# Sharing the samples' input projection with the prompt's, moving each second expert choice into the next window, and spreading the samples' last dots

## The reference

```
c -> modulation (6*1024 columns per layer, for the prompt and each sample)
h = RMSNorm(x) * (1 + scale1) + shift1
p = h @ w_in                                  (1024 x 3592, split into the three mixers' inputs)
A: dilated window attention, 4 heads x 64     (samples: against a cache of 2048 rows)
B: gated delta rule, 4 heads x 128, causal conv of width 4 on q/k/v
C: stick-breaking attention, 4 heads x 64     (samples: 16 cache pages of 128 rows each)
x += gate1 * (concat(A, B, C) @ w_out)
h2 = RMSNorm(x) * (1 + scale2) + shift2
q = h2 @ wq;  8 heads, scores against 2 x 128 keys, top 16 of 128 twice, top 16 of 256
x += gate2 * sum over 128 picks of softmax * gelu(h2 . u[idx]) * v[idx]     (16384 experts)
```

## Time and profile before

| what | value |
|---|---|
| runs of the kernel before | 4712.13, 4719.75, 4724.38 us; median 4719.75 |
| profiled execution | 4694.12 us, span of its instructions 4692.3 us |
| busy shares over the span | PE 73%, DVE 61%, POOL 55%, ACT 19% |
| moved by DMA | 1401.7 MB, mean 299 GB/s; gathers and other indirect loads 1107.4 MB of it |
| mean granted PE clock | 0.843 of full speed |

### The profile page before, as it was taken

One profiled execution on the slowest core, in us unless ns is written; L12 is line 12 of the kernel. 1 busy time (PEld: TensorE's weight loads), 2 busy tenths in 40 slices (PEclk: granted clock), 3 DMA queues, 4 the chain that ended last, 5 costly groups with the idle time before them and its releaser, 6 DMA issues. The chain is left out here.

```text
span 4692.3 us, 42307 instructions
## 1 busy us (share of the span) xinstructions
PE 3425.7 (73%) x11982; PEld 1910.2 (41%) x11982; DVE 2843.8 (61%) x5777; ACT 877.2 (19%) x2045; POOL 2587.5 (55%) x2244
## 2 busy tenths in 40 slices
PE   5966768539298889575887967498898436748897
PEld 2624543126154554262455426255553113213351
DVE  1225552556866648787774688868649767584322
ACT  1113110011142112112321211242221011000120
POOL 0000362025767757687774667777656767665563
PEclk8986789759589999796998988799999767869896
DMA  6451375549989989899998889999988989999995
GB/s 229 139 180 56 101 227 177 187 104 320 354 318 345 385 308 339 331 399 342 366 376 320 306 334 395 353 346 361 367 306 308 378 303 348 362 382 377 336 330 154
DMA packets 586674, 1401.71 MB, mean 299 GB/s; under 512 B 67314, under 2 KB 287659, under 8 KB 585244
## 3 DMA queue, kind: packets, MB, share of 16 engines
q0 software_dynamic: 306176, 1107.44, 63.6%
q1 hardware_dynamic: 261836, 274.77, 17.7%
q10 hardware_dynamic: 18432, 16.79, 1.1%
HBM read 1387.11 MB, written 11.88 MB: 298 GB/s over the span
## 5 line engine op out<-in xcount | busy, mean ns | idle before, releaser
L2496 PE MATMUL bank<-arena 128*128 128x512 f32 (+1 forms) x3264 | 1589.6, 636 | 200.5 <-PEq L2493 117.9
L2392 POOL DMA_INDIRECT arena<-in_peer_u_dram,arena x1056 | 1279.6, 1212 | 693.2 <-issue 303.1
L2392 POOL DMA_INDIRECT arena<-in_peer_v_dram,arena x1056 | 1160.5, 1099 | 749.2 <-PE bank L2496 448.4
L2442 DVE CUSTOM_DVE_ANT_0 arena<-arena 128x1024 f32<-128x1024 f32 (+1 forms) x1056 | 1269.8, 1224 | 447.5 <-DMA arena<-in_peer_u_dram,arena 417.4
L2496 PEld LDWEIGHTS bank<-arena 128*128 128x128 f32 (+1 forms) x3264 | 614.8, 196 | 1013.6 <-issue 869.5
L2479 ACT ACTIVATE arena<-arena 128x128 f32<-128x128 f32 (+1 forms) x816 | 301.5, 394 | 1072.9 <-PE bank L2496 686.1
L2458 DVE SCALAR_TENSOR_TENSOR arena<-arena 128x1024 f32<-128x1024 f32 x232 | 297.6, 1283 | 243.6 <-DMA arena<-in_peer_v_dram,arena 223.3
L799 PE MATMUL bank<-arena 128*128 128x256 f32 (+3 forms) x1472 | 368.9, 414 | 101.0 <-PEq L792 95.9
L2138 POOL DMA_INDIRECT arena<-in_cache_sb_k_dram,arena x64 | 84.0, 1312 | 550.4 <-POOLq L2131 530.2
L799 PEld LDWEIGHTS bank<-arena 128*128 128x128 f32 (+1 forms) x1472 | 247.0, 170 | 220.8 <-issue 156.1
L641 PE MATMUL bank<-arena 128*9 128x512 f32 x384 | 180.3, 627 | 66.9 <-PEq L637 45.9
(11 more groups left out here) (339 smaller groups left out, 3730.0 us busy)
## 6 DMA issues: line engine op xcount, KB each, us to landing
arena<-in_w_in_dram SPq DMA_DIRECT2D x78, 1024.0 KB, 13.2
arena<-in_w_ada_dram SPq DMA_DIRECT2D x24, 2048.0 KB, 8.4
arena<-in_w_out_dram SPq DMA_DIRECT2D x24, 1024.0 KB, 13.0
arena<-in_peer_wq_dram SPq DMA_DIRECT2D x24, 1024.0 KB, 15.0
arena<-in_peer_u_dram,arena POOLq DMA_INDIRECT x1056, 7.4
arena<-in_peer_v_dram,arena POOLq DMA_INDIRECT x1056, 6.2
arena<-in_cache_sb_k_dram SPq DMA_DIRECT2D x128, 128.0 KB
arena<-in_cache_sb_v_dram SPq DMA_DIRECT2D x128, 128.0 KB
```

The lines of the kernel that those rows point to most:

```text
L2392: pool_.indirect_dma_start(G_[g % GR][0:b.parts, :], None, tables[0 if which == "u" else 1], bass.IndirectOffsetOnAxis(ap=b.index[:, n:n + ...
L2442: vec.tensor_tensor_reduce(row, row, b.h, 1.0, 0.0, ALU.mult, ALU.add, b.AV[0:b.parts, n:n + 1]).then_inc(freed_by_dve, 1)
L2496: last = pe_.matmul(ps[6 + i][0:b.rows, :], DG[owners[g][1] % NDG][0:b.parts, 0:b.rows], G_[g % GR][0:b.parts, i * GBLK:(i + 1) * GBLK], s ...
```

## The change

- **Shared projection.** `project(u, m, s)` takes a sample unit along: h of the 8 samples stands in 8 more columns of the prompt's HT, feature groups become 264 columns wide, and each of the eight other chunks gets one more group of 8 rows. The samples' own `project` and its loads of w_in are gone. Layer 0's samples ride with unit 0 in the first window; layer 1's ride with unit 3 in W3, where the results go over three staging buffers into a DRAM tensor `ROWS`, and come back in W4 by `rows_back`. A stage `sample_norm` of weight 8 stands ahead in W3. The features of mixer B stay in `BF` and are transposed to rows at the start of `delta_sample` (three more ticks, weight 80 for 75).
- **Second choice.** The prompt's lane keeps one `choose_tile` (tile a). That of tile b runs in the next window as a lane of its own, over the first 0.22 of its steps.
- **First window.** `sample_norm` runs over 0 to 0.02 of the window, `rest` over 0.02 to 0.25 (beside the projection), then `after_lane` makes the samples wait for the prompt's projection, and the samples' other stages take 0.255 to 1. `late` is one stage of 24 chunks of 256 columns (1 MB, ring of four) beside the one `choose_tile`, with weight 80. The projection weighs 120 where samples ride along.
- **Rows on DVE.** In a phase with one list only (rows alone in W1 to W3), every second row from the eighth on goes to DVE (`ON_DVE_ALONE = 2`), 60 rows instead of 30.
- **W4.** The samples' lane takes 0.7 of the window instead of 0.85, and the samples' 16 dots are spread between the 128 rows of the last tile instead of following them.
- `TMP` and `CWR` of the prompt's projection leave the score buffer SC[1], which the second choice now reads at that time.

```diff
+ON_DVE_ALONE = 2
 def on_dve(b, n):
-    return not b.sample and n >= FIRST_ON_DVE and n % ON_DVE == ON_DVE - 1
+    return not b.sample and n >= FIRST_ON_DVE and n % b.every == b.every - 1
...
-            def project(u, m):
+            def project(u, m, s=None):
...
+                wide = n_ + NB if s else n_
-                        mine = [(c, kind, i) for i in range(nt)]
+                        mine = [(c, kind, i) for i in range(nt)] + ([(c, kind, "sample")] if s else [])
...
+                        if spill and t - 2 in of_samples:
+                            sp_.wait_ge(act2sp, 1).then_inc(act2sp, -1)
+                            sp_.dma_start(ROWS[:, lo:hi], s.m.STAGE[k % 3][:, 0:hi - lo]).then_inc(k_landed[k % 3], 16)
...
-                                    last = pe_.matmul(ps[t % BANKS][:, 0:n_], m.W[c % ring][:, k, off:off + P], m.HT[:, k, 0:n_],
+                                    last = pe_.matmul(ps[t % BANKS][:, 0:wide], m.W[c % ring][:, k, off:off + P], m.HT[:, k, 0:wide],
+                                elif i == "sample":
+                                    last = pe_.matmul(ps[t % BANKS][0:NB, 0:hi - lo], m.HT[:, k, n_:wide],
+                                                      m.W[c % ring][:, k, 0:hi - lo], start=(k == 0), stop=(k == KD - 1))
...
+                                act_.copy(s.m.BF[:, f, :], bank[:, n_:wide])
...
+            def rows_back(u, m):
+                def sp():
+                    for dst, lo, hi in ((m.PZ[0:NB, 0, :], 2304, 2816), (m.BA[0:NB, 0, :], 2816, 2824), (m.QKC[0:NB, 0, :], 2824, 3336),
+                                        (m.VC[0:NB, 0, :], 3336, 3592), (m.QKA[0:NB, 0, :], 0, 512), (m.VA[0:NB, 0, :], 512, 768)):
+                        sp_.dma_start(dst, ROWS[:, lo:hi]).then_inc(loaded, 16)
+                    yield
+                    sp_.wait_ge(loaded, 96).then_inc(loaded, -96)
+                    yield
+                return 2, {"sp": sp}
...
+            def after_lane(it, stages):
+                def waits(eng):
+                    def program():
+                        eng.wait_ge(it.stage_over, 4 * stages)
+                        yield
+                    return program
+                return 1, {"sp": waits(sp_), "pe": waits(pe_), "act": waits(act_), "dve": waits(vec)}
...
-                    return [paced(begin, 8), paced(project(u, m), 80), paced(heads(u, m), 14)] + between + [paced(delta_sample(u, m), 75),
+                    return [paced(heads(u, m), 14), paced(delta_sample(u, m), 80),
...
-                        paced(choose_tile(u, e, 0, meanwhile[0:1]), 59), paced(choose_tile(u, e, 1, meanwhile[1:2]), 59)]
+                        paced(choose_tile(u, e, 0, meanwhile), 80 if meanwhile else 59)]
...
+                        b.every = ON_DVE_ALONE if len(phase) == 1 else ON_DVE
...
+        def second_choice(u, span):
+            ticks, programs = LC.choose_tile(u, None, 1)
+            return [span[0] + (span[1] - span[0]) * (n + 1) / ticks for n in range(ticks)], programs
...
-        late = [LP.modulate(1, tiles, GBLK, half * MOD // 2, (half + 1) * MOD // 2) for half in range(2)]
+        late = [LP.modulate(1, [AR.room(KD, GBLK // 2) for _ in range(4)], GBLK // 2)]
...
+        window(LP.token_mixers(units[0], m, own, late),
+               [([paced(LS.sample_norm(samples[0], rooms[0][0], m.HT), 8)], 0.0, 0.02), ([paced(rest, 50)], 0.02, 0.25), (rest_of_samples, 0.255, 1.0)], [])
...
+            choice = second_choice(u, (0.0, 0.22))
...
-                window([], LS.token_mixers(samples[1], (LAST_at, arena_cols)), phases + [[("u", s)], [("v", s)]], (0.0, 0.85))
+                of_sample = [paced(LS.rows_back(samples[1], rooms[1][0]), 4)] + LS.token_mixers(samples[1], rooms[1])
+                window([], [(of_sample, 0.0, 0.7)], phases[:-1] + [phases[-1] + [("u", s)], [("v", s)]], choice)
```

More of the change, by code:

```diff
@@ L745, in project @@
                 tap = {i: f for f, i in feature_at.items()}
-                BANKS = 2 if u.sample else 4
+                of_samples = [i for i, g in enumerate(groups) if g[2] == "sample"]
+                spill = s is not None and s.m.STAGE is not None
+                BANKS = 4
                 ring = len(m.W)
                 ticks = len(groups) + 3
-                T = None if u.sample else m.TMP
+                T = m.TMP
                 def destinations(g):
@@ L808, in act @@
                         g = t - 1
-                        if g == 0 and not u.sample:
+                        if g == 0:
                             act_.wait_ge(dve2act, 1).then_inc(dve2act, -1)
@@ L834, in dve @@
                     for t in range(ticks):
-                        if t == 0 and not u.sample:
+                        if t == 0:
                             if u.first:
@@ L1875, in dve @@
                 def dve():
-                    for t in range(ticks):
+                    for t in range(-ahead, ticks):
                         if t == 2:
@@ L2292, in token_mixers @@
                             paced(queries_sample(u, e), 35), paced(choose_tile(u, e), 20)]
-                return [paced(begin, 14), paced(project(u, m), 102), paced(unit_lengths(u, m), 31), paced(heads(u, m), 19),
+                begin = norm(u, 0, m.H1, m.HT, m.SEG, m.SQJ, m.SMALL, first_w)
+                before = [paced(sample_norm(s.u, m, m.HT), 8)] if s is not None and s.normed is None else []
+                return before + [paced(begin, 14), paced(project(u, m, s), 120 if s else 102), paced(unit_lengths(u, m), 31), paced(heads(u, m), 19),
                         paced(attend_a(u, m), 18 + 6 * u.t0), paced(attend_c(u, m), 41 + 20 * u.t0), paced(delta_chunks(u, m), 30),
@@ L2356, in experts @@
             batches = [b for phase in phases for which, b in phase if which == "v"]
+            for phase in phases:
+                for which, b in phase:
+                    if which == "v":
+                        b.every = ON_DVE_ALONE if len(phase) == 1 else ON_DVE
             number = Walked.batches
@@ L2575, in build @@
                 phases = [[("u", s)], [("v", s)]] + phases
+            choice = second_choice(u, (0.0, 0.22))
             if k < 3:
-                window(LP.token_mixers(units[k + 1]), [], phases)
+                own = None
+                if k == 2:
+                    own = Room()
+                    own.u, own.m, own.normed = samples[1], rooms[1][0], None
+                window(LP.token_mixers(units[k + 1], prompt_room(units[k + 1]), own), [], phases, choice)
             else:
```

125 lines of the change are left out of this document (82 added, 43 removed).

## The result

The changed kernel takes 4777.05 us (median of 4 runs, 4767.02 to 4798.44) against 4715.94 us for the kernel before on the same chip: a ratio of 1.0149, interval 1.0121 to 1.0177. It is slower by 1.5%, clear of the spread of the runs; 4524 us were forecast, with a range of 4420 to 4650 and 0.07 for slower. The profiled execution is 4768.71 us long, its span 4766.9 us, 74.6 us above the span before.

What follows compares the result with a forecast made beforehand. Limits differ by phase: DMA in dots alone with DVE close behind, DMA in mixed, PE in rows alone. First window -84, W1 to W3 -30, W4 -82 sum to -196: 4524 us median, range 4420 to 4650.

Steps and rivals of the forecast that it cites:

- +45: Dots alone of W1 to W3: the second choice's 55 us on DVE lengthens them by 0, 20 and 25 us.
- I take -20: W4, dots and mixed: less traffic and DVE's 30 us hole closed, but choice and `delta_sample` fill dots: -20, between 0 and -29.
- DVE becomes the bound: Rival: each choice lies whole on top of the dots and the mixed phases win nothing; 4784 us, chance 0.07.
- +10: Rows alone of W1 to W3: 235, 222, 246 us against 229.8, 222.5, 242.1, +10 in all; bounds -105 and +40.
- -85: Mixed phases of W1 to W3: 256 gathers at 1.49 us make 381 us each, -30, -35, -20; bounds -120 and 0.
- Rows alone: -62: W4: the samples' chain leaves PE, gathers take 185 us where rows and samples' dots took 225.7 + 21.5: -62.
- -84: Whole first window: projection, middle and end together 84 us shorter.
- -6 for -7: First window, projection: with `rest` beside it 203 us for 260, -57, but +50 for stages losing their cover: -7.
- -57 for -67: First window, end: one choice leaves and `late` sets 176 us for 243, -67, between -98 and +25.
- -10, between 0 and -40: First window, middle: the samples' chain is further along and takes in more of the pages, 10 us less.
- now it comes from rows at 1.00: W4's end: PE comes from rows, no longer waiting for dots; the end stays 80 us, 27 less by the skill's rule.
- DMA at its best rate: Rival: PE no longer holds buffers, so rows alone take 200 us and mixed 370; 4399 us, chance 0.10.

Runs made afterwards that it cites:

- The weight of 118: Changed kernel with the one choice in the lanes of W1 to W3 weighing 118, not 59, and `late` in 12 chunks of 512 columns; 4767.28 us, 1.0116.
- e5: Changed kernel with both choices in the prompt's lane, half of `late` beside each, every fourth row on DVE, W4's old order; 4651.6 us, 0.9891.
- e2: Changed kernel with the second choice back behind the first in the prompt's lane, the rest kept; 4767.88 us, 1.0112.
- the fillers: Changed kernel without second choice, 24 idle DVE instructions in its place: two inputs 4776.69 us (1.0138), one input 4749.72 us (1.0097).

## Why the prediction was wrong

**Dots alone, the largest error: the term "+45" (W1 0, W2 +20, W3 +25), and in W4 "I take -20".** The busy time of DVE was right within 12 us in each window; what failed is the sentence "W1 ... lies under the 229.6 it had", and the same step elsewhere: DVE's idle time was taken as room for the choice. In W2 and W3 the prediction put a phase at DVE's busy time and some 7 us; it is the busy time and 26 and 31 us, in W1 and W4 50 and 39. With the choice left out 38 to 48 us are idle in a phase; with it 26 to 50 are. About half of the idle time is the landing of the first gather, the flush of the samples and the waits of the convolution and the samples' stages, which hold back everything behind them in DVE's order; the rest is short gaps between instructions. The measured price is 37 to 49 us for a choice of 55, 167 in the four windows. Instructions without purpose cost 137 to 166, and half of them more than half of that. So the rival "DVE becomes the bound" (4784) came closest to the time and had 0.07. It was near in the price of a choice, for which it had 55. That its time was met is partly luck: it left out the mixed phases' gain of 85 us, which came, and it did not foresee the 63 us more of rows alone, the 100 of W4 and the 42 of the first window.

**Rows alone, "+10" for +73.** The order "until the choice begins PE sets the pace" was right, and so was, within 12 us, the second part under the choice. The first part was forecast 28 or 29 us too short in each window. In W1 and W3 most of that is idle time of PE, 22 and 21 us, which had been put at nothing; in W2 43 rows fall before the choice instead of 38 (PE spends 80.7 us on rows, not 68), 18.8 us of `out_projection` instead of a third, and PE is idle for 10 us in a stretch that had been taken as full.

**Mixed, "-85", right to the us**, but it was no gain of the window. The weight of 118 puts `out_projection` back into the mixed phase: that phase grows by as much as rows alone falls. Mixed and rows alone together were 641, 638 and 644 us before and are 639, 624 and 649 after, 12 us less in all, although a choice of 55 us had left each of them. The DMA share over the two phases together is 0.90 to 0.93 before, after and with the weight of 118; that this is why their sum hardly moves is argued from the rows, not shown.

**W4.** Its parts, in us in all:

| choice in front | lane | samples' dots | W4 |
|---|---|---|---|
| yes | 0.7 | spread | 1066 |
| yes | 0.85 | behind | 1027 |
| no | 0.7 | spread | 1022 |
| no | 0.7 | behind | 1031 |
| no | 0.85 | behind | 994 |
| before: own projection, no choice | 0.85 | behind | 1048 |

In the kernels with 1027 and 1031 every second of the last rows goes to DVE, in the other kernels every fourth, so the parts are good to some us only. "Rows alone: -62" was -45, and it is real; but the chain that leaves the rows comes to stand in the dots and mixed phases, which the step left at -20. Without the choice the draw-in with the spread dots costs 27 us (1022 for 994), the choice 33 to 45. The shared projection with what stays of the change gives 54 us in W4 and costs 34 in W3. There the dots alone, where the wider projection stands, grow by 7 us and the two phases after it by 27; what lengthens those two was not tried.

**First window, "-84" for -42.** The projection (-6 for -7) was right in its sum only: with `rest` beside it, it took 184 us (77 to 261) instead of 203, and the stages behind it gave the difference back, which is luck. The end (-57 for -67) was right, but not by the finer chunks, since 12 chunks of 2 MB in one stage gave 177 us for 180. Before, `late` stood in two stages and issued no load between 805 and 878 us; that gap is gone with the one stage. The middle was wrong: "-10, between 0 and -40" is +21. With the choices back it is 425 us in e5 as in the changed kernel, but 401 in e2, against 404 before; these two differ there in the place of `late` and one weight. So it matters how the stages are placed; which of them makes the middle longer stays open.

**The two rules.** Two inputs from SBUF on DVE do cost POOL time, as the Trainium skill (GPSIMD Engine Reference, section 8, Key points) says: +0.18 us a gather between the fillers in W2, some 29 us in four windows. The second choice itself did not do it: a gather takes 1.30, 1.35, 1.36 and 1.41 us in the four dots alone of the changed kernel and 1.25, 1.34, 1.30 and 1.45 without the choice, so the 0.1 us more a gather that the prediction's sentence on the rule had is not seen, nor its 30 us.

In the last stretch of W4, 82 us for 80 before, the granted clock is 0.55 for 0.50. PE came from rows at 0.96, worked on for some us and then stood still for 9.7 us, until the first row of the samples could be summed; behind that it was busy without a gap at 0.50, the lower of the two levels:

```profile
4695.00:4700.00 5.00, 0.00 (x0) 0.00 (x0) 4.47 (x6) 0.21 (x1) 3.78 (x5) 0.50 1.04 209
4705.00:4720.00 15.00, 15.00 (x19) 2.29 (x18) 0.00 (x0) 1.35 (x5) 3.57 (x4) 0.50 0.27 74
```

So the step "now it comes from rows at 1.00" did not hold: PE had a pause in front of the end after all. The row still speaks against the rule of the Trainium skill (TensorE: Matmul & The Clock Gate, Part 1) that sustained activity releases the throttle.

**A slip in a rival.** In "DMA at its best rate" the sum does not follow from its terms: rows alone 703 - 600 and mixed 3 x 11 are 136 us, not 125. Nothing hangs on it.

## What to carry to other kernels

Idle time of an engine beside a phase is room for other work only if the waits that make it can be overtaken: before an addition is costed as hidden, list what ends each wait, and take away the landing of the first transfer, whatever stands at the head of the engine's order, and the short gaps between instructions. Where a lane of stages is spread over a window by weights, taking one stage out moves all others later; the sum over the phases that they move between has to be costed, not each phase alone. A change made of several parts is best split: here the shared projection with finer loads is worth 1.1% (0.9891), and the other parts together cost more than that (1.0149 in all). The parts act on each other: moving the choice back alone changed next to nothing (1.0112), and two choices and 60 rows then met on DVE in rows alone.

## What the runs showed of the hardware

A gather instruction on POOL is held back by DVE's instructions with two inputs from SBUF. The two fillers show it most plainly, since each of their instructions lasts 2.28 or 2.29 us. Of the gathers that began in a filler at least 0.95 us before its end, all 109 beside one input last 0.89 to 0.96 us, and all 85 beside two inputs 1.90 to 3.06. In the changed kernel it can be more. Gathers near the end of W4's dots alone:

```profile
3980.47 4.47 POOL L2468 DMA_INDIRECT arena<-in_peer_u_dram,arena  x1 [0.30 <-issue]
3985.24 5.62 POOL L2468 DMA_INDIRECT arena<-in_peer_u_dram,arena  x1 [0.30 <-issue]
3991.16 0.94 POOL L2468 DMA_INDIRECT arena<-in_peer_v_dram,arena  x1 [0.30 <-issue]
```

DVE at the same time; the dots (line 2518) have two inputs from SBUF, line 2118 one from SBUF and one from PSUM:

```profile
3980.62 1.21 DVE L2518 CUSTOM_DVE_ANT_0 arena<-arena 128x1024 f32<-128x1024 f32 x1
...
3982.91 1.21 DVE L2518 CUSTOM_DVE_ANT_0 arena<-arena 128x1024 f32<-128x1024 f32 x1
...
3984.06 0.27 DVE L2118 TENSOR_TENSOR arena<-arena,bank 128x128 f32<-128x128 f32 x1
3984.26 1.21 DVE L2518 CUSTOM_DVE_ANT_0 arena<-arena 128x1024 f32<-128x1024 f32 x1
```

A gather that otherwise takes 0.94 us lasts 4.47 us here; it ends at 3984.94, soon after the short instruction of line 2118, and the next one lasts 5.62 us beside dots without such a pause. The Trainium skill (SBUF — State Buffer, Who interferes with whom) states the mechanism: a DVE instruction with two SBUF inputs contends with a GpSimd instruction that reads SBUF. The trace agrees, and shows that a dense row of such instructions can hold a gather for several of them.
